# The first stage of a one-core attention layer: products of a cleared tile ahead of it, x's first tile in four loads, and loads issued when earlier ones have landed

## The chip, the cores and the metric

The kernel runs on one core of one Trainium2 chip. The metric is device microseconds of an execution, median of several. A core has TensorE (PE: matrix products; PEld in the profile is its weight load), VectorE (DVE), ScalarE (ACT), GpSimd (POOL) and SyncE (SP, which here only issues DMA transfers). ACT issues a few DMA transfers too.

## The reference, cut to what matters

x is 1024 tokens by 1024 features in float32. One projection gives queries, keys and values of three kinds of attention and a gate; each attention's output is normalised, gained, multiplied by the silu of the gate and projected back, and a layer norm of `alpha*x + y` ends it:

```python
h = jnp.einsum('bsd,de->bse', x, w_in[l]) + b_in[l]
qa, ka, va, qb, kb, vb, qc, z = jnp.split(h, split_idx, axis=-1)
mkv = jnp.einsum('bmd,de->bme', mem, w_mem[l])      # 256 memory tokens
y = jnp.concatenate([rms(oa), rms(ob), rms(oc)], -1) * g_branch[l] * silu(z)
x = layer_norm(DEEPNORM_ALPHA * x + y @ w_out[l], ln_gain[l], ln_bias[l])
```

Only the start of the projection is touched by the change: the product of x with the 256 columns of `vb`.

## The kernel before, in words

Every large float32 product is made of three: an operand is split into a high part (ACT rounds it: `x_hi`, `w_hi`, `mem_hi`, `g_hi`) and a low part (DVE subtracts: `x_lo`, `w_lo`, `mem_lo`), and PE adds hi*hi, hi*lo and lo*hi. The raw value and the low part share their memory.

**The first stage** is `first_chunk` (lines 680 to 701). The features are cut into KT = 8 tiles of 128. For each tile k PE goes over the 8 blocks of 128 tokens and issues three products of 128x256 each, so 24 products a tile and 192 in all, into four banks at once (`first_ps`). It waits ahead of each tile's weight piece (`FIRST_PIECES`: tiles 0, 1, 2-3, 4-7) and ahead of each half of x's tile, for both the rounding and the split. SP loads x as 16 pieces of 256 KB (two halves of each tile) with no wait between them (line 543); ACT issues the four weight pieces first of all (line 920), then loads its table of functions (L922).

**SP's queue behind x**, in this order (lines 544 to 551): chunk 1's weights (two of 512 KB, `load_chunk`), `ident`, `rope`, two broadcasts into `b_row`, chunk 2's weights (1 MB), `mem_raw` (1 MB), and, behind a wait for the end of the first stage, chunk 3's weights. All of these are one queue.

**ACT and DVE behind x**: ACT rounds chunk 1 (`kva`, from x), chunk 2 (`mk`, from the memory tokens) and the memory tokens (`memory_hi`). DVE makes the low parts in the same order (`chunk_lo(1)`, `chunk_lo(2)`, `memory_lo`), and only then runs `finish_first` (line 1131), which reads the first stage's four banks into `v_b`, and after that the jobs.

**The jobs** (`plan.steps`): PE computes one job after the other (`project`, lines 733 to 735 for a block of x, 24 products each), here job 0, job 1, keys 0, job 2, keys 1 and so on. `transpose_keys` (L749) waits for `keys_rotated`, which DVE gives at the end of `finish_keys` (L1215 to L1233) of that block. So the first transposition needs: `mem_raw` landed, `mem_hi`, `mem_lo`, `v_b`, and block 0's keys, in the order in which DVE has them written out.

Of the kernel before, what the change touches and what calls it, by code (L numbers as in the profile page):

```python
# [34 lines left out]
F32R = mybir.dt.float32r  # L35
ALU = mybir.AluOpType
ACT = mybir.ActivationFunctionType
AX = mybir.AxisListType

P = 128  # L40
SEQ = 1024
DM = 1024
MEM = 256
NB = SEQ // P
NBM = MEM // P
KT = DM // P
# [12 lines left out]
C = 256  # L59
HALF = 512  # L60
# [23 lines left out]
def units():  # L84

    out = []
    for i in range(NB):
# [6 lines left out]
        else:  # L94
# [8 lines left out]

GATE_ITERATIONS = 2
FIRST_PIECES = ((0, 1), (1, 2), (2, 4), (4, 8))
PREPARED = {3: (4, (5, 6, 6, 7)), 4: (8, (9, 9, 10, 10)), 5: (11, (11, 11, 12, 12)), 6: (13, (13, 13, 14, 14)),
            7: (18, (18, 19, 19, 20)), 8: (22, (22, 23, 23, 24)), "g0": (26, (27, 27)), "g1": (27, (28, 28))}
QS = 4
# [174 lines left out]
def layer(nc, x, x_t, mem_t, w_qkv, w_gate, w_mem, b_in, sinks, g_branch, w_out, ln_gain, ln_bias,  # L283
# [5 lines left out]
    with ExitStack() as ctx:  # L289
        def sem(name):  # L290
            return ctx.enter_context(nc.semaphore(name))
# [5 lines left out]
        spilled = [sem(f"spilled{s}") for s in range(2)]  # L297
        turned_keys_in, q_in = sem("turned_keys_in"), [sem(f"q_in{s}") for s in range(QS)]
        wo_in, ln_in = [sem(f"wo_in{k}") for k in range(FT)], sem("ln_in")
        x_in = [[sem(f"x_in{k}{h}") for h in range(2)] for k in range(KT)]  # L300
        first_in, mem_in = [sem(f"first_in{m}") for m in range(len(FIRST_PIECES))], sem("mem_in")
        chunk_in = [[sem(f"chunk_in{s}{h}") for h in range(2)] for s in range(3)]
        gate_in = [sem(f"gate_in{s}") for s in range(2)]
# [7 lines left out]
        x_rounded, chunk_rounded, chunk_split = sem("x_rounded"), sem("chunk_rounded"), sem("chunk_split")  # L311
        x_split, first_rounded, first_split = sem("x_split"), sem("first_rounded"), sem("first_split")
# [27 lines left out]
        def at(name, shape, dt, offset):  # L340
            return nc.alloc_sbuf_tensor_at(name, shape, dt, offset=offset)
# [7 lines left out]
        def nbytes(*shape):  # L349
            return 4 * int(np.prod(shape))  # L350
# [4 lines left out]
        x_hi = at("x_hi", [P, KT, SEQ], F32R, r_x.base)  # L355
        x_raw = at("x_raw", [P, KT, SEQ], F32, lo_half)
        x_lo = at("x_lo", [P, KT, SEQ], F32R, lo_half)
# [35 lines left out]

        r_t = Region(nbytes(2 * SEQ) + QS * nbytes(2, 2, P))
        prob = [at(f"prob{s}", [P, SEQ], F32, r_t.base + s * nbytes(SEQ)) for s in range(2)]
        spill = [at(f"spill{s}", [P, 2, 2, C], F32R, r_t.base + s * nbytes(SEQ)) for s in range(2)]
        q_at = r_t.base + nbytes(2 * SEQ)
        q_pair = [at(f"q_pair{s}", [P, 2, 2 * P], F32R, q_at + s * nbytes(2, 2, P)) for s in range(QS)]
# [45 lines left out]
        wide = [ctx.enter_context(nc.psum_tensor(f"wide{b}", [P, HALF], F32)) for b in range(3)]  # L444
# [5 lines left out]
        def f32(ap):  # L450
            return ap.bitcast(F32)
# [5 lines left out]
        def slot_of(c):  # L457
            return (c + 2) % 3
# [60 lines left out]
        def _(sp):  # L519
# [17 lines left out]
                sp.dma_start(g_raw[f % 2][:, :, :], w_gate[f]).then_inc(gate_in[f % 2], 16)  # L537


            for k in range(KT):  # L540
                for h in range(2):
                    cols = slice(h * HALF, (h + 1) * HALF)
                    sp.dma_start(x_raw[:, k, cols], x_t[k * P:(k + 1) * P, cols]).then_inc(x_in[k][h], 16)  # L543
            load_chunk(1)
            sp.dma_start(ident[:, :], ident_d).then_inc(ident_in, 16)
            sp.dma_start(rope[:, :, :], rope_d.rearrange("(b p) d -> p b d", p=P)).then_inc(rope_in, 16)
# [130 lines left out]

        @block.tensor
        def _(pe):
            def first_chunk():  # L680

                s = slot_of(0)
                for k in range(KT):
                    for m, (lo, _) in enumerate(FIRST_PIECES):
                        if lo == k:
                            pe.wait_ge(first_rounded, m + 1)
                            pe.wait_ge(first_split, m + 1)
                    for i in range(NB):
                        if i % (NB // 2) == 0:
                            pe.wait_ge(x_rounded, 2 * k + i // (NB // 2) + 1)  # L690
                            pe.wait_ge(x_split, 2 * k + i // (NB // 2) + 1)
                        cols = slice(i * P, (i + 1) * P)
                        dst = first_ps[i // 2][:, (i % 2) * C:(i % 2 + 1) * C]
                        pe.matmul(dst, x_hi[:, k, cols], w_hi[s][:, k, :], start=(k == 0 and i % 2 == 0),
                                  stop=False, skip_group_check=True)
                        pe.matmul(dst, x_hi[:, k, cols], w_lo[s][:, k, :], start=False, stop=False,
                                  skip_group_check=True)
                        mm = pe.matmul(dst, x_lo[:, k, cols], w_hi[s][:, k, :], start=False, stop=(k == KT - 1),
                                       skip_group_check=True)
                        if k == KT - 1 and i % 2:  # L700
                            mm.then_inc(first_full, 1)
# [36 lines left out]
            def transpose_keys(k):  # L738
# [10 lines left out]
                    t = pe.transpose(bank[:, h * P:(h + 1) * P], twice, ident[:, :])  # L749
                t.then_inc(narrow_full, 1)  # L750

            first_chunk()
            pe.wait_ge(ident_in, 16)
            for what, n in plan.steps:
# [161 lines left out]

        @block.scalar
        def _(act):
            for m, (lo, hi) in enumerate(FIRST_PIECES):
                act.dma_start(w_raw[slot_of(0)][:, lo:hi, :], w_qkv[COL_VB // C, :, lo:hi, :])\  # L920
                   .then_inc(first_in[m], 16)
            nc.scalar.preload_act_table_set("natural_log_exp_and_others")  # L922

            def chunk_hi(c):
# [9 lines left out]
                act.wait_ge(first_in[m], 16)  # L934
                act.activation(w_hi[s][:, k, :], w_raw[s][:, k, :], ACT.Copy).then_inc(first_rounded, 1)

            def x_hi_half(k, h):
                cols = slice(h * HALF, (h + 1) * HALF)
                act.wait_ge(x_in[k][h], 16)
                act.activation(x_hi[:, k, cols], x_raw[:, k, cols], ACT.Copy).then_inc(x_rounded, 1)  # L940

            def memory_hi():
                act.wait_ge(mem_in, 16)
# [34 lines left out]
            for k in range(KT):  # L978
                for m, (lo, _) in enumerate(FIRST_PIECES):
                    if lo == k:  # L980
                        first_hi(m)
                for h in range(2):
                    x_hi_half(k, h)
            chunk_hi(1)
            chunk_hi(2)
            memory_hi()
# [75 lines left out]
            for v in range(ITERATIONS):  # L1062
# [8 lines left out]
                f, since = divmod(v, 2 * GATE_ITERATIONS)  # L1071
# [4 lines left out]
                for i in stage_at(v, NORM_AT):  # L1076
                    s = i % 2
                    cols = slice(0, DM if i < NB - 1 else POOL_COLS)
# [5 lines left out]
                for i, j in stage_at(v, YSPLIT_AT):  # L1084
                    n = plan.narrow["y", i, j]
                    act.wait_ge(narrow_read[n % 2], n // 2 + 1)
                    f = slice(BRANCH_TILES[j][0], BRANCH_TILES[j][-1] + 1)
# [11 lines left out]
        def _(dve):  # L1099
# [4 lines left out]
                dve.tensor_tensor(w_lo[s][:, k, :], w_raw[s][:, k, :], f32(w_hi[s][:, k, :]), ALU.subtract)\  # L1104
                   .then_inc(first_split, 1)

            def x_lo_half(k, h):
                cols = slice(h * HALF, (h + 1) * HALF)
                dve.wait_ge(x_rounded, 2 * k + h + 1)
                dve.tensor_tensor(x_lo[:, k, cols], x_raw[:, k, cols], f32(x_hi[:, k, cols]), ALU.subtract)\  # L1110
                   .then_inc(x_split, 1)

            def chunk_lo(c, q):
# [122 lines left out]
            for k in range(KT):  # L1236
                for m, (lo, _) in enumerate(FIRST_PIECES):
                    if lo == k:
                        first_lo(m)
                for h in range(2):  # L1240
                    x_lo_half(k, h)
            for q in range(4):
                chunk_lo(1, q)
            for q in range(4):
# [120 lines left out]
            for v in range(ITERATIONS):  # L1365
# [8 lines left out]
                for i, j in stage_at(v, Y_AT):  # L1374
                    n, bank = bank_of(narrow, plan.narrow, ("y", i, j))
# [5 lines left out]
                for i in stage_at(v, NORM_AT):  # L1381
# [4 lines left out]
                    if i == NB - 1:  # L1386
                        cols = slice(POOL_COLS, DM)
# [6 lines left out]
                for half in range(2):  # L1394
                    for i in stage_at(v, RES_AT[half]):
                        cols = slice(half * HALF, (half + 1) * HALF)
# [10 lines left out]
                for i, j in stage_at(v, SCALE_AT):  # L1407
                    lo, n = BRANCHES[j]
# [8 lines left out]
        @block.gpsimd  # L1417
        def _(pool):
            def gate_lo(f):
                pool.wait_ge(gate_rounded, f + 1)  # L1420
                pool.tensor_tensor(g_lo[f % 2][:, :, :], g_raw[f % 2][:, :, :], f32(g_hi[f % 2][:, :, :]),  # L1421
                                   ALU.subtract).then_inc(gate_split, 1)

            for v in (v_a, v_b, v_c):
                pool.memset(v[:, :, :, HD:VW], 1.0).then_inc(ones_set, 1)
            for v in range(ITERATIONS):
                for i, j in stage_at(v, YSPLIT_AT):
                    pool.wait_ge(y_rounded, 3 * i + j + 1)
                    f, cols = slice(BRANCH_TILES[j][0], BRANCH_TILES[j][-1] + 1), slice(i * P, (i + 1) * P)
                    pool.tensor_tensor(y_lo[:, f, cols], zt[:, f, cols], f32(y_hi[:, i, f, :]), ALU.subtract)\  # L1430
                        .then_inc(y_split, 1)
                for i in stage_at(v, NORM_AT):
                    s = i % 2
                    cols = slice(0, DM if i < NB - 1 else POOL_COLS)
                    if i == 0:
                        pool.wait_ge(ln_in, 32)
                    pool.wait_ge(normed, i + 1)
                    pool.tensor_tensor(res[s][:, cols], res[s][:, cols], gain[:, cols], ALU.mult).then_inc(gained, 1)
                    pool.wait_ge(gained, i + 1)
                    pool.tensor_tensor(res[s][:, cols], res[s][:, cols], bias[:, cols], ALU.add).then_inc(finished, 1)  # L1440
                f, since = divmod(v, 2 * GATE_ITERATIONS)
                if since == GATE_ITERATIONS and 1 <= f < FT - 1:
                    gate_lo(f + 1)
# [73 lines left out]
```

## Time and profile before

| | us |
|---|---|
| median of 3 runs | 530.27 |
| the three runs | 530.27, 525.37, 530.83 |
| profiled execution, its own time | 525.63 |
| profiled execution, its span | 523.7 |
| PE busy in the span | 500.3 (96%) |
| DVE, ACT, POOL busy | 314.4, 226.0, 72.8 |

The span goes from the first instruction to the last; the execution's own time is 1.93 us longer. Views of the profile used below: the page (shares of the engines, the clock that was granted, the chain of work that ended last), the timeline of one engine, the sum of each engine's waits, the chain of waits in order of time, and the table of stretches of the span with the DMA engines' busy share and the rate that they moved. Products overlap in the timeline: the time that one takes out of PE's is the distance between two starts.

### The profile page before, as it was taken

How to read it: one execution, taken by the hardware profiler on the slowest of the kernel's cores; microseconds unless marked ns; L12 is line 12 of the kernel's file. 1: busy time of each engine (PE TensorE's matmuls, PEld its weight loads, DVE VectorE, ACT ScalarE, POOL GpSimd, SP SyncE). 2: the span in 40 equal slices, each digit the busy share in tenths (PEclk: the TensorE clock that was granted, in tenths of full speed). 3: DMA queues.
4: the chain of work that ended last, by engine and by line, in shares of the span. 5: the costliest groups of instructions: out<-in, count | busy, mean ns of one | idle time of the engine just before them, and what ended most of it. 6: DMA issues, size and time to landing. Idle time of an engine off the chain costs nothing.

```text
span 523.7 us, 9727 instructions
## 1 busy us (share of the span) xinstructions
PE 500.3 (96%) x3504; PEld 459.2 (88%) x3504; DVE 314.4 (60%) x872; ACT 226.0 (43%) x504; POOL 72.8 (14%) x53
## 2 busy tenths in 40 slices
PE   4999999999999989999999889999999999999993
PEld 4999999999999878888888778888888888998982
DVE  4786545467666434344535488876867676776534
ACT  5622212021212055554555478464547364454530
POOL 0000000000000001101111010241414140311415
PEclk9999999999999989999999999999999999999998
DMA  8952453467522543323213496133232324141022
GB/s 289 375 191 37 154 176 128 148 209 235 181 101 81 162 115 107 100 82 103 85 48 93 154 257 228 59 97 97 96 92 86 105 61 143 49 134 40 11 72 80
DMA packets 50030, 66.26 MB, mean 127 GB/s; under 512 B 9280, under 2 KB 39616, under 8 KB 49984
## 3 DMA queue, kind: packets, MB, share of 16 engines
q1 hardware_dynamic: 49408, 64.60, 39.2%
q10 hardware_dynamic: 576, 1.05, 0.6%
q8 instruction: 29, 0.48, 0.4%
q14 instruction: 17, 0.14, 0.1%
HBM read 50.41 MB, written 15.20 MB: 125 GB/s over the span
## 4 chain that ended last, share of the span: by engine, by line
PE 86%; DVE 4%; SPq 3%; DMA 3%; ACT 2%; issue 1%; POOLq 0%; POOL 0%; DVEq 0%; ACTq 0%
PE long_ps L889 16%; PE o_ps L856 13%; PE wide L722 7%; PE wide L724 7%; PE wide L723 7%; PE narrow L839 5%; PE long_ps L799 5%; PE long_ps L801 5%; PE long_ps L800 5%; PE wide L827 4%; PE wide L828 4%; DMA mem_raw<-in_mem_t 2%; PE narrow L866 2%; SPq L543 1%; PE wide L733 1%; PE wide L735 1%
## 5 line engine op out<-in xcount | busy, mean ns | idle before, releaser
L722 PE MATMUL wide<-x_hi,w_hi 128*128 128x256 f32 x320 | 88.5, 277 | 0.2
L723 PE MATMUL wide<-x_lo,w_hi 128*128 128x256 f32 x320 | 88.3, 276 | 0.0
L724 PE MATMUL wide<-x_hi,w_lo 128*128 128x256 f32 x320 | 88.3, 276 | 0.0
L722 PEld LDWEIGHTS wide<-x_hi,w_hi 128*128 128x128 f32 x320 | 60.1, 188 | 0.5 <-issue 0.5
L723 PEld LDWEIGHTS wide<-x_lo,w_hi 128*128 128x128 f32 x320 | 60.1, 188 | 0.0
L724 PEld LDWEIGHTS wide<-x_hi,w_lo 128*128 128x128 f32 x320 | 60.1, 188 | 0.0
L1043 ACT ACTIVATE prob_t<-narrow 128x512 f32<-128x512 f32 (+3 forms) x68 | 32.7, 505 | 56.1 <-PE narrow L839 56.0
L970 ACT ACTIVATE spill<-turn 128x512 fp32r<-128x512 f32 x21 | 13.3, 633 | 98.5 <-DVE turn L1188 72.7
L889 PE MATMUL long_ps<-wo_hi,y_hi 128*128 128x512 f32 x128 | 53.2, 416 | 0.0
L889 PE MATMUL long_ps<-wo_lo,y_hi 128*128 128x512 f32 x128 | 52.3, 409 | 0.0
L1421 POOL TENSOR_TENSOR g_lo<-g_raw,g_hi 128x1024 fp32r<-128x1024 f32 x6 | 14.3, 2386 | 272.1 <-ACT g_hi L975 272.1
L889 PE MATMUL long_ps<-wo_hi,y_lo 128*128 128x512 f32 x128 | 51.7, 404 | 0.0
L839 PE MATMUL narrow<-ident,prob 128*128 128x128 f32 x272 | 43.1, 274 | 4.1 <-ACT prob L1028 4.1
L799 PE MATMUL long_ps<-x_hi,g_hi 128*128 128x512 f32 x112 | 46.9, 419 | 0.0
L1028 ACT ACTIVATE prob<-prob,nb 128x128 f32<-128x128 f32 (+7 forms) x40 | 27.5, 698 | 39.8 <-DVE nb L1337 36.3
L801 PE MATMUL long_ps<-x_hi,g_lo 128*128 128x512 f32 x112 | 44.5, 398 | 0.0
L800 PE MATMUL long_ps<-x_lo,g_hi 128*128 128x512 f32 x112 | 44.5, 397 | 0.0
L1430 POOL TENSOR_TENSOR y_lo<-zt,y_hi 128x256 fp32r<-128x256 f32 (+1 forms) x24 | 22.1, 921 | 149.8 <-ACT y_hi L1088 149.8
L1028 ACT ACTIVATE prob<-wide,nb 128x128 f32<-128x128 f32 (+1 forms) x88 | 30.9, 406 | 20.5 <-DVE nb L1302 12.7
L856 PEld LDWEIGHTS o_ps<-v_b,prob_t 128*128 128x128 f32 x288 | 37.0, 191 | 2.7
L1354 DVE RECIPROCAL rden<-o_ps 128x1 f32<-128x1 f32 (+1 forms) x48 | 8.0, 166 | 50.1 <-PE o_ps L856 50.1
L839 PEld LDWEIGHTS narrow<-ident,prob 128*128 128x128 f32 x272 | 31.8, 140 | 5.9 <-ACT prob L1028 4.7
(151 smaller groups left out, 1204.4 us busy)
## 6 DMA issues: line engine op xcount, KB each, us to landing
q_spill<-spill SPq DMA_DIRECT2D x32, 256.0 KB, 2.5
q_pair<-q_spill SPq DMA_DIRECT2D x128, 64.0 KB, 2.0
w_raw<-in_w_qkv SPq DMA_DIRECT2D x12, 512.0 KB, 5.7
x_raw<-in_x_t SPq DMA_DIRECT2D x16, 256.0 KB, 7.9
g_raw<-in_w_gate SPq DMA_DIRECT2D x8, 512.0 KB, 3.5
q_pair<-q_spill SPq DMA_DIRECT2D x32, 128.0 KB, 2.7
q_pair<-q_spill SPq DMA_DIRECT2D x128, 32.0 KB, 1.8
wo_raw<-in_w_out SPq DMA_DIRECT2D x8, 512.0 KB, 4.6
```

Of the source, the lines that this page charges most:

```text
L722: pe.matmul(dst, w_hi[s][:, k, f], t_hi[:, k, cols], start=(k == 0), stop=False)
L723: pe.matmul(dst, w_hi[s][:, k, f], t_lo[:, k, cols], start=False, stop=False)
L724: mm = pe.matmul(dst, w_lo[s][:, k, f], t_hi[:, k, cols], start=False, stop=(k == KT - 1))
L799: pe.matmul(dst, g_hi[f % 2][:, k, :], x_hi[:, k, cols], start=(k == 0), stop=False)
L800: pe.matmul(dst, g_hi[f % 2][:, k, :], x_lo[:, k, cols], start=False, stop=False)
L801: mm = pe.matmul(dst, g_lo[f % 2][:, k, :], x_hi[:, k, cols], start=False, stop=(k == KT - 1))
L839: t = pe.transpose(bank[:, j * P:(j + 1) * P], prob[u % 2][:, col:col + P], ident[:, :])
L856: mm = pe.matmul(o_ps[:, at_col:at_col + VW], prob_t[w][:, col % HALF:col % HALF + P], v_tile(u, t, hh), start=(t == mine[0][0]), stop=(t ...
L889: mm = pe.matmul(long_ps[half][:, :], y, w[:, k, half * HALF:(half + 1) * HALF], start=(k == 0 and p == 0), stop=(n == half_done[half]))
L1028: e = act.activation(prob[s][:, cols], src, ACT.Exp, bias=nb[:, r, hh:hh + 1])
L1043: act.activation(prob_t[w % 4][:, 0:size], bank[:, 0:size], ACT.Copy).then_inc(narrow_read[n % 2], 1)
L1430: pool.tensor_tensor(y_lo[:, f, cols], zt[:, f, cols], f32(y_hi[:, i, f, :]), ALU.subtract)\
```

## The change

Six edits, all in the first stage. (1) POOL clears a tile `blank` of 128x256 ahead of its three other memsets, and PE, after a wait for that, issues 19 products of that tile into bank `wide0`, which the first job overwrites later. (2) x's tile 0 is loaded in four pieces of 128 KB rather than two of 256 KB; tiles 1 to 7 stay in halves, so SP issues 18 loads rather than 16. (3) Ahead of the loads of tile k, for k of 2 and more, SP waits until all pieces of tile k-2 have landed. (4) ACT issues weight pieces 0 and 1 first, piece 2 after the rounding of tile 0 and piece 3 after that of tile 1. (5) ACT and DVE round and split by the new pieces. (6) PE waits for a piece's rounding ahead of its first product, for the weight piece's low part ahead of the second, and for x's low part ahead of the third, where it waited for all of these ahead of the first.

```diff
+X_PIECES = [(0, lo, lo + C) for lo in range(0, SEQ, C)] \
+    + [(k, lo, lo + HALF) for k in range(1, KT) for lo in range(0, SEQ, HALF)]
+WARM_UP = 19
...
+        blank = at("blank", [P, C], F32R, r_t.base)
...
-            for k in range(KT):
-                for h in range(2):
-                    cols = slice(h * HALF, (h + 1) * HALF)
-                    sp.dma_start(x_raw[:, k, cols], x_t[k * P:(k + 1) * P, cols]).then_inc(x_in[k][h], 16)
+            for n, (k, lo, hi) in enumerate(X_PIECES):
+                if k >= 2 and lo == 0:
+                    for older, piece in enumerate(X_PIECES):
+                        if piece[0] == k - 2:
+                            sp.wait_ge(x_in[older], 16)
+                sp.dma_start(x_raw[:, k, lo:hi], x_t[k * P:(k + 1) * P, lo:hi]).then_inc(x_in[n], 16)
             load_chunk(1)
...
+            def warm_up():
+
+                pe.wait_ge(zeroed, 1)
+                for _ in range(WARM_UP):
+                    pe.matmul(wide[0][:, 0:C], blank[:, 0:P], blank[:, :], start=True, stop=True)
...
-                    for m, (lo, _) in enumerate(FIRST_PIECES):
-                        if lo == k:
-                            pe.wait_ge(first_rounded, m + 1)
-                            pe.wait_ge(first_split, m + 1)
+                    m = next((m for m, (lo, _) in enumerate(FIRST_PIECES) if lo == k), None)
+                    if m is not None:
+                        pe.wait_ge(first_rounded, m + 1)
                     for i in range(NB):
-                        if i % (NB // 2) == 0:
-                            pe.wait_ge(x_rounded, 2 * k + i // (NB // 2) + 1)
-                            pe.wait_ge(x_split, 2 * k + i // (NB // 2) + 1)
+                        n = piece_at.get((k, i * P))
+                        if n is not None:
+                            pe.wait_ge(x_rounded, n + 1)
...
+                        if i == 0 and m is not None:
+                            pe.wait_ge(first_split, m + 1)
                         pe.matmul(dst, x_hi[:, k, cols], w_lo[s][:, k, :], start=False, stop=False,
                                   skip_group_check=True)
+                        if n is not None:
+                            pe.wait_ge(x_split, n + 1)
...
+            warm_up()
             first_chunk()
...
-            for m, (lo, hi) in enumerate(FIRST_PIECES):
+            def load_first(m):
+                lo, hi = FIRST_PIECES[m]
                 act.dma_start(w_raw[slot_of(0)][:, lo:hi, :], w_qkv[COL_VB // C, :, lo:hi, :])\
                    .then_inc(first_in[m], 16)
+
+            load_first(0)
+            load_first(1)
             nc.scalar.preload_act_table_set("natural_log_exp_and_others")
...
-                for h in range(2):
-                    x_hi_half(k, h)
+                for n, piece in enumerate(X_PIECES):
+                    if piece[0] == k:
+                        x_hi_piece(n)
+                if k + 2 < len(FIRST_PIECES):
+                    load_first(k + 2)
...
+            pool.memset(f32(blank[:, :]), 0.0).then_inc(zeroed, 1)
             for v in (v_a, v_b, v_c):
                 pool.memset(v[:, :, :, HD:VW], 1.0).then_inc(ones_set, 1)
```

## Rows read from the trace of the kernel before

**Rows 1.** the page: busy time by engine, granted clock, and the chain that ended last.

```profile
PE 500.3 (96%) x3504; PEld 459.2 (88%) x3504; DVE 314.4 (60%) x872; ACT 226.0 (43%) x504; POOL 72.8 (14%) x53
...
PEclk9999999999999989999999999999999999999998
...
PE 86%; DVE 4%; SPq 3%; DMA 3%; ACT 2%; issue 1%; POOLq 0%; POOL 0%; DVEq 0%; ACTq 0%
```

**Rows 2.** timeline of PE, first stage and after: start us, duration us, engine, line, operation.

```profile
6.92 0.55 PE L694 MATMUL long_ps<-w_hi,x_hi 128*128 128x256 f32 x1 [6.92 <-DVE x_lo L1110]
...
12.17 0.28 PE L694 MATMUL long_ps<-w_hi,x_hi 128*128 128x256 f32 x1
...
31.22 0.28 PE L733 MATMUL wide<-w_hi,x_hi 128*128 128x256 f32 x1
...
36.55 0.28 PE L735 MATMUL wide<-w_hi,x_lo 128*128 128x256 f32 x1
37.08 0.44 PE L749 MATMUL narrow<-ident,keys 128*128 128x128 f32 x2 [0.26 <-DVE keys L1233]
```

**Rows 3.** waits of PE over the whole span: who for whom, us in total, times, longest.

```profile
PE narrow L839 <- ACT prob L1028: 4.1, 2, 2.7
```

**Rows 4.** the chain of waits in order of time, 0 to 60 us: start us, us, what.

```profile
11.34 5.80 SPq L547
...
18.61 10.95 DMA mem_raw<-in_mem_t
29.59 1.07 ACT mem_hi L946
...
33.18 2.40 DVE v_b L1136 x4
...
36.60 0.44 DVE keys L1233
```

**Rows 5.** stretches of the span, all engines, granted clock, DMA share, GB/s.

```profile
0.00:6.00 6.00, 0.00 (x0) 0.00 (x0) 0.42 (x1) 2.17 (x3) 0.46 (x7) 1.00 0.58 161
6.00:17.00 11.00, 10.08 (x67) 10.11 (x68) 9.11 (x15) 9.19 (x17) 0.00 (x0) 1.00 1.04 394
17.00:28.00 11.00, 11.00 (x99) 11.00 (x99) 6.91 (x12) 5.59 (x7) 0.00 (x0) 1.00 1.04 357
28.00:29.50 1.50, 1.50 (x15) 1.50 (x15) 1.29 (x2) 0.00 (x0) 0.00 (x0) 1.00 0.05 16
```

**Rows 6.** timeline of SP's DMA queue.

```profile
0.74 8.41 SPq L543 DMA_DIRECT2D x_raw<-in_x_t  x16
9.19 0.97 SPq L529 DMA_DIRECT2D w_raw<-in_w_qkv  x2
```

**Rows 7.** timeline of ACT, first stage.

```profile
5.11 0.42 ACT L935 ACTIVATE w_hi<-w_raw 128x256 fp32r<-128x256 f32 x1 [1.20 <-DMA w_raw<-in_w_qkv]
5.43 1.25 ACT L940 ACTIVATE x_hi<-x_raw 128x512 fp32r<-128x512 f32 x2
...
9.33 0.63 ACT L940 ACTIVATE x_hi<-x_raw 128x512 fp32r<-128x512 f32 x1 [1.05 <-DMA x_raw<-in_x_t]
```

**Rows 8.** timeline of DVE, low parts of the second chunk's weights.

```profile
20.15 2.64 DVE L1116 TENSOR_TENSOR w_lo<-w_raw,w_hi 128x512 fp32r<-128x512 f32 x4
```

**Rows 9.** DMA issues of the page, and x_raw by tile.

```profile
g_raw<-in_w_gate SPq DMA_DIRECT2D x8, 512.0 KB, 3.5
...
DMA to landing us min/median/max: 4.2/7.9/9.2
```

**Rows 10.** timeline of POOL, its memsets of the same kind.

```profile
0.79 0.16 POOL L1425 MEMSET v_b<- 128x64 f32 x1
```

**Rows 11.** timeline of PE, its last product.

```profile
515.24 0.40 PE L889 MATMUL long_ps<-wo_hi,y_lo 128*128 128x512 f32 x1
```

**Rows 12.** stretches of the span behind that product.

```profile
520.50:521.00 0.50, 0.00 (x0) 0.00 (x0) 0.00 (x0) 0.00 (x0) 0.50 (x1) 0.73 0.00 0
521.00:521.50 0.50, 0.00 (x0) 0.00 (x0) 0.00 (x0) 0.00 (x0) 0.15 (x1) 0.50 0.39 158
```

More of the change, by code:

```diff
@@ L299, in layer @@
         wo_in, ln_in = [sem(f"wo_in{k}") for k in range(FT)], sem("ln_in")
-        x_in = [[sem(f"x_in{k}{h}") for h in range(2)] for k in range(KT)]
+        x_in = [sem(f"x_in{n}") for n in range(len(X_PIECES))]
+        zeroed = sem("zeroed")
         first_in, mem_in = [sem(f"first_in{m}") for m in range(len(FIRST_PIECES))], sem("mem_in")
@@ L679, in _ @@
         def _(pe):
+            def warm_up():
+                pe.wait_ge(zeroed, 1)
+                for _ in range(WARM_UP):
+                    pe.matmul(wide[0][:, 0:C], blank[:, 0:P], blank[:, :], start=True, stop=True)
             def first_chunk():
                 s = slot_of(0)
+                piece_at = {(k, lo): n for n, (k, lo, _) in enumerate(X_PIECES)}
                 for k in range(KT):
-                    for m, (lo, _) in enumerate(FIRST_PIECES):
-                        if lo == k:
-                            pe.wait_ge(first_rounded, m + 1)
-                            pe.wait_ge(first_split, m + 1)
+                    m = next((m for m, (lo, _) in enumerate(FIRST_PIECES) if lo == k), None)
+                    if m is not None:
+                        pe.wait_ge(first_rounded, m + 1)
                     for i in range(NB):
-                        if i % (NB // 2) == 0:
-                            pe.wait_ge(x_rounded, 2 * k + i // (NB // 2) + 1)
-                            pe.wait_ge(x_split, 2 * k + i // (NB // 2) + 1)
+                        n = piece_at.get((k, i * P))
+                        if n is not None:
+                            pe.wait_ge(x_rounded, n + 1)
                         cols = slice(i * P, (i + 1) * P)
@@ L935, in first_hi, with x_hi_piece @@
                 act.activation(w_hi[s][:, k, :], w_raw[s][:, k, :], ACT.Copy).then_inc(first_rounded, 1)
[L937 to L940, printed above, removed]
+            def x_hi_piece(n):
+                k, lo, hi = X_PIECES[n]
+                act.wait_ge(x_in[n], 16)
+                act.activation(x_hi[:, k, lo:hi], x_raw[:, k, lo:hi], ACT.Copy).then_inc(x_rounded, 1)
             def memory_hi():
@@ L1105, in first_lo, with x_lo_piece @@
                    .then_inc(first_split, 1)
[L1107 to L1110, printed above, removed]
+            def x_lo_piece(n):
+                k, lo, hi = X_PIECES[n]
+                dve.wait_ge(x_rounded, n + 1)
+                dve.tensor_tensor(x_lo[:, k, lo:hi], x_raw[:, k, lo:hi], f32(x_hi[:, k, lo:hi]), ALU.subtract)\
                    .then_inc(x_split, 1)
@@ L1239, in _ @@
                         first_lo(m)
-                for h in range(2):
-                    x_lo_half(k, h)
+                for n, piece in enumerate(X_PIECES):
+                    if piece[0] == k:
+                        x_lo_piece(n)
             for q in range(4):
```

## The prediction

> **What bounds the kernel now.** The page first: PE is busy for 96% of the span and holds 86% of the chain that ended last, yet SP's queue and DMA hold 3% each [rows 1]. PE's timeline shows two speeds in the first stage: 24 products lie between 6.92 and 12.17, 0.219 us apart, and the other 168 between there and 31.22, 0.1134 us apart [rows 2]: the 1.2 GHz and the 2.4 GHz level. The granted-clock column reads 1.00 over both [rows 5], so at the start I go by the distances. From 31.22 PE does jobs 0 and 1, ends them at 36.83 (36.55 + 0.28), and waits 0.26 us for block 0's rotated keys [rows 2].
>
> That small wait matters. The chain in order of time passes not through the first stage's products but through SP's queue, the landing of `mem_raw`, its rounding at 29.59, `v_b` at 33.18 and the keys at 36.60 [rows 4]. DVE has `memory_lo` and `finish_first` written ahead of the first keys, so the transposition at 37.08 comes 7.5 us after `mem_raw` is there, whatever PE has done. Two bounds end within 0.3 us of each other here: PE's own work and the DMA engines. These moved 161 GB/s to 6.0, then 394 and 357 GB/s at a full share until 28.0, then next to nothing [rows 5]; `mem_raw` is used 1.6 us after they fall silent. Behind 37.1 PE is the bound to the end: its longest wait there is 2.7 us and its waits are few [rows 3].
>
> **The change, part by part.**
>
> *Warm-up.* POOL's memset of 64 columns takes 0.16 us [rows 10]. One of 256 columns is between that and four times that, 0.64; I take 0.4 (a fixed part is likely), so PE starts near 1.3. 19 products at 0.219 us end at 5.5. If the clock rises after as much work as before (5.25 us), it rises at 6.5. These products cost nothing: PE was idle to 6.92, and the bank is overwritten later.
>
> *Four pieces and split waits.* The weight's rounding started at 5.11 and took 0.42, x's two halves took 1.25 [rows 7]. A quarter takes about 0.35, so the first product can start at 6.0 rather than 6.92; with half the traffic ahead of it perhaps 0.8 earlier. Two products at half speed and 190 at 0.1134 give a stage that ends at 28.0: 3.2 us earlier (3.0 to 4.0). The next weights' low parts were done at 22.79 (20.15 + 2.64) [rows 8], so jobs 0 and 1 follow at once even if these come 4 us later, and PE stands at the first keys at 33.6.
>
> *Two more loads on SP* cost 2 x 0.53 us of issue (8.41 / 16) [rows 6], in SP's new waits. ACT's two moved issues, likely as long as SP's, lie between roundings. Late tiles have room: PE needs tile 7 at 25.3, and by the sum below it lands at about 19. Tile 2 is tight (needed at 11.7; it lands near 9.5, and three roundings of some 0.6 us leave it whole at 11.3); a stall of up to 1 us there is covered by the wait at the first keys. Should that cover be gone, it costs what it is.
>
> *SP's waits.* This is the edit that counts. Queued behind x's loads on SP are chunk 1, `ident`, `rope`, `b_row` twice, chunk 2 and `mem_raw`; the last one's reader is on the path. Up to the last byte of x and of the first weights there are 5.24 MB; before, they were through at 16.8 (6.0 x 161 + 10.8 x 394 GB/s), and the 4.0 MB behind them needed until 28.0 [rows 5]. After the change at most two tiles of x are under way. A cycle from a tile's landing to that of the tile two later: two issues 0.53 apart; a fixed part of 2.17, from the 3.5 us of a 512 KB load [rows 9] less 0.52 MB / 394 GB/s; 0.67 for the second half: 3.37, and I take 3.6 since the other tile's bytes share the engines. Tile 0 lands near 5.9 (its second half's rounding was the later half of the 1.25 us from 5.43). Tile 1's was rounded at 9.33 [rows 7], with 0.77 MB of weight pieces alongside that now come later: 7.4. So tiles 3, 5 and 7 are issued at 7.4, 11.0 and 14.6; tile 7 lands at 18.2, its last byte 1.5 before that, 16.7. The two late weight pieces (0.77 MB, 1.95 us) fall half into gaps: +1.0, so 17.7 to 17.8 against 16.8. From there the engines are full as before, so `mem_raw` and the first transposition come **1.0 us later**. The ends: with no gaps and the engines at 394 GB/s from 2.0 instead of the 232 that 161 over 6.0 comes to, 1.6 earlier; with a cycle of 4.7 (0.53 and x's shortest landing of 4.2 [rows 9]), tile 7 is issued at 16.8 and the shift is 4.2 later. I take 1.0, since the 512 KB loads are nearest in kind, and keep both ends. Here the Trainium skill speaks against the edit (DMA: Bandwidth & Descriptors, Anatomy of one DMA): each transfer has about 2.0 us of fixed time that its size doesn't change. By that figure the cycle would be 3.2 and the keys 0.3 us earlier, no loss at all; the measured 2.17 stands against it, and the wait is what exposes it.
>
> SP's issue of the rest is no new bound: `mem_raw` was issued 9.4 us after chunk 1, of which 5.8 were one blocked issue [rows 4, 6]. From 15.7 that gives 25.1 if it blocks again and 19.3 if not; its bytes are due near 26.
>
> **The sum.** Start and warm-up: -3.2 at the end of the stage, all of it turned into waiting at the first keys; those keys +1.0. The span goes from 523.7 to 524.7, and the execution's own time from 525.63 to 526.6. The median of the three runs is 4.6 above the profiled execution, so I add the 1.0 there: 531.3. The idle stretch at the first keys grows from 0.26 to 0.26 + 3.2 + 1.0 = 4.5 us.
>
> **The rivals.** *A: the clock falls in that stretch (the slower side).* After the last product (515.24 + 0.40 = 515.64 [rows 11]) the granted clock fell within 520.50 to 521.00, at 520.73 by its mean of 0.73 [rows 12]: 5.1 us after PE stopped. After the 2.7 us wait nothing is slower on the page [rows 1, 3]. 4.5 us lies between, nearer to 5.1. If it falls, the jobs behind the wait run 5.25 us at half speed, as at the start, which loses 24 x 0.106 = 2.5 us, on a path where PE is the bound: +3.5, 533.8; with the keys 2 us later, 534.8. It decides from an idle stretch of about 5 us, that is from a shift of 1.6, and with luck of timing below that. The Trainium skill (TensorE: Matmul & The Clock Gate, The HAM clock gate) has half speed as the default to which an idle engine goes back, which names this mechanism.
>
> *B: the gain goes through.* For that `mem_raw` would have to land earlier, or DVE not hold the keys. At its earliest (-1.6) it gives 528.7; the whole -3.2 (527.1) would need the chain to be misread, for which the 0.26 us wait, named after DVE's keys, leaves little room.
>
> *C: loads in turn starve the stage or delay the keys by 2.3 to 4.2*, clock held: 532.6 to 534.5.
>
> *D: the change doesn't do what it says*: the clock isn't up at the first true product. The stage would then end up to 2.5 us later, at 30.5, still ahead of the keys: the same 531.3, with a shorter idle stretch. It lies within the forecast.
>
> **How the numbers follow.** Forecast with D, 0.45 (shift -0.5 to +2.3, 529.8 to 532.6); A 0.30; B 0.15; C 0.10. The range has to hold these and the spread of the runs shown (525.4 to 530.8, so a median can lie 4 us lower for that alone): 526.0 to 535.5. It leaves out a low median with a gain, and C with A. 1% is 5.3 us, about what can be told from no change; no case alone reaches it on the faster side, so 0.10 for B with the runs' spread. Slower by as much takes A with C, or A with the spread: 0.12. Within: 0.78.
>
> **What would show it.** Right: 19 products of `blank` from about 1.3; first true product near 6.0, 0.113 us apart soon after; first job at about 28; DMA engines with gaps between 7 and 17; `mem_hi` at 30 to 32; a wait of PE at the first keys, for DVE, of 4 to 5 us; that transposition at about 38; behind it PE as before. A shows as products 0.21 to 0.22 us apart behind the wait, for some 5 us. It would be wrong if `mem_raw` landed clearly before 29, or PE's wait stayed under 2 us, or if what lies behind the first keys changed its length.

## The result, and the profile after

The change makes the kernel slower. The median is 539.75 us (536.69 to 542.19, 6 runs) against 527.82 (524.94 to 531.71, 6 runs); the ratio is 1.0201 [1.0157, 1.0245], some 10.6 us (1.0201 times 527.82; the two medians lie 11.9 apart). I had forecast 1.0 us more than before, 531.3, and a range up to 535.5. Ratios here and below are of fast runs alone; three slow ones of the kernel before, one of 1606 us, are left out.

The page of the changed kernel: span, busy time, and the chain's shares, to be held against [rows 1].

```profile
span 539.2 us, 9763 instructions
...
PE 510.6 (95%) x3523; PEld 469.0 (87%) x3523; DVE 314.7 (58%) x874; ACT 226.4 (42%) x506; POOL 73.1 (14%) x54
...
PE 85%; DMA 6%; DVE 4%; ACT 2%; SPq 2%; issue 1%; POOLq 0%; POOL 0%; DVEq 0%; ACTq 0%
```

PE's share stays near 95%, and DMA's share of the chain doubles from 3% to 6%. PE's waits over the whole span name the place at once; columns as in [rows 3].

```profile
PE narrow L766 <- DVE keys L1258: 10.5, 1, 10.5
...
PE wide L750 <- ACT w_hi L951: 0.6, 1, 0.6
```

The wait for the first rotated keys, 0.26 us before [rows 2], is 10.5 us. In the chain in order of time, up to that wait, one sees where it comes from; [rows 4] has the same view of before.

```profile
3.07 4.07 DMA x_raw<-in_x_t
...
7.58 6.57 DMA x_raw<-in_x_t
...
14.58 4.97 DMA x_raw<-in_x_t
...
20.46 0.44 SPq L534
...
25.42 13.16 DMA mem_raw<-in_mem_t
...
38.60 1.06 ACT mem_hi L968
...
45.61 0.44 DVE keys L1258
```

A second half of tile 1 issued at 3.07 lands at 7.14 and releases tile 3; tile 3's lands at 14.15 and releases tile 5; tile 5's lands at 19.55 and releases tile 7. Only then, at 20.46, does chunk 1 leave SP (9.19 before [rows 6]). `mem_raw` is issued at 25.42 and used at 38.60, against 29.59 [rows 4], and the keys come 9.0 us later, 7.5 us behind `mem_raw` as before. The stretches show the DMA engines part idle to 27 where they had been full [rows 5] (last three columns: granted clock, DMA share, GB/s):

```profile
6.00:12.00 6.00, 5.76 (x46) 5.58 (x46) 3.06 (x7) 3.07 (x7) 0.00 (x0) 1.00 0.80 264
12.00:17.00 5.00, 4.77 (x39) 4.58 (x40) 3.79 (x7) 3.56 (x6) 0.00 (x0) 1.00 0.80 265
17.00:22.00 5.00, 5.00 (x46) 5.00 (x46) 3.52 (x7) 2.53 (x4) 0.00 (x0) 1.00 0.63 206
22.00:27.00 5.00, 5.00 (x46) 5.00 (x46) 1.63 (x3) 1.23 (x2) 0.00 (x0) 1.00 0.86 248
27.00:32.00 5.00, 4.42 (x38) 4.25 (x37) 2.58 (x4) 2.12 (x2) 0.00 (x0) 1.00 1.01 312
32.00:37.00 5.00, 3.59 (x31) 3.38 (x29) 2.59 (x4) 2.12 (x2) 0.00 (x0) 1.00 1.06 383
```

PE itself did what was meant. Its timeline: warm-up at 1.10, first true product at 5.32 rather than 6.92 [rows 2], products 0.118 us apart from 6.8 on, a stall at tile 2, and the last product of the first stage at 28.84 (31.11 before). The first job waits for chunk 1's rounding until 29.70.

```profile
1.10 4.42 PE L691 MATMUL wide<-blank 128*128 128x256 f32 x19 [1.10 <-POOL blank L1450]
5.32 0.41 PE L707 MATMUL long_ps<-w_hi,x_hi 128*128 128x256 f32 x1
...
12.02 0.36 PE L707 MATMUL long_ps<-w_hi,x_hi 128*128 128x256 f32 x1 [0.25 <-ACT x_hi L962]
```

```profile
28.84 0.28 PE L715 MATMUL narrow<-w_hi,x_lo 128*128 128x256 f32 x1
29.70 0.36 PE L750 MATMUL wide<-w_hi,x_hi 128*128 128x256 f32 x1 [0.58 <-ACT w_hi L951]
```

```profile
46.09 0.69 PE L766 MATMUL narrow<-ident,keys 128*128 128x128 f32 x2 [10.51 <-DVE keys L1258]
```

The transposition of the first keys is at 46.09 (37.08 before), and the granted clock has fallen meanwhile (third column from the end):

```profile
35.00:40.00 5.00, 0.59 (x5) 0.38 (x4) 2.18 (x4) 1.95 (x3) 0.00 (x0) 1.00 1.05 391
40.00:45.00 5.00, 0.00 (x0) 0.00 (x0) 4.98 (x10) 0.61 (x1) 0.00 (x0) 0.58 0.47 88
45.00:50.00 5.00, 3.91 (x19) 3.91 (x20) 2.81 (x11) 0.39 (x1) 0.00 (x0) 0.50 0.18 49
50.00:55.00 5.00, 5.00 (x41) 5.00 (x41) 2.31 (x9) 0.57 (x2) 0.00 (x0) 0.89 0.00 0
```

From start times of the same instruction in both traces: the last product of the first stage is 2.3 us earlier than before, the first transposition 9.0 later, the product 60 places on 11.3 later. So 2.3 us are lost to half speed behind the wait. The profiled execution of after is 15.5 us longer than that of before; 4.1 of these come between 64 and 190 us, where PE issues its products at one of two paces, whatever the kernel (last section), and are not the change's. 9.0 + 2.3 = 11.3 us are, and the timed ratio says 10.6.

### The profile page after: what moved, and what is told of

Its sections match the earlier page's. It is cut to its first block, busy times and chain, and to the rows that moved or that the text cites. A ratio compares the mean times of both kernels' runs of the same rounds, so it can differ in the third digit from the quotient of the medians.

```text
span 539.2 us, 9763 instructions
## 1 busy us (share of the span) xinstructions
PE 510.6 (95%) x3523; PEld 469.0 (87%) x3523; DVE 314.7 (58%) x874; ACT 226.4 (42%) x506; POOL 73.1 (14%) x54
## 4 chain that ended last, share of the span: by engine, by line
PE 85%; DMA 6%; DVE 4%; ACT 2%; SPq 2%; issue 1%; POOLq 0%; POOL 0%; DVEq 0%; ACTq 0%
PE long_ps L907 16%; PE o_ps L874 12%; PE wide L741 7%; PE wide L739 7%; PE wide L740 7%; PE narrow L857 5%; PE long_ps L817 5%; PE long_ps L819 5%; PE long_ps L818 4%; PE wide L845 4%; PE wide L846 4%; DMA x_raw<-in_x_t 3%; DMA mem_raw<-in_mem_t 2%; PE narrow L884 2%; PE wide L750 2%; PE wide L751 2%
## 5 line engine op out<-in xcount | busy, mean ns | idle before, releaser
L741 PE MATMUL wide<-x_hi,w_lo 128*128 128x256 f32 x320 | 89.6, 280 | 0.0
L992 ACT ACTIVATE spill<-turn 128x512 fp32r<-128x512 f32 x21 | 13.3, 632 | 103.0 <-DVE turn L1213 76.1
```

What stands on the lines that cost most here:

```text
L741: mm = pe.matmul(dst, w_lo[s][:, k, f], t_hi[:, k, cols], start=False, stop=(k == KT - 1))
```

## The experiments

Two theories after the result. **W**: SP's waits delay everything queued behind x; `mem_raw` is ahead of the first keys in DVE's order; the clock falls in the wait that opens. **R**: the warm-up, the small loads or the late weight pieces cost the time. "Keys" below is the start of the first key transposition.

| kernel | `mem_hi` starts | keys | median us | ratio to before |
|---|---|---|---|---|
| before | 29.59 | 37.08 | 527.82 to 530.68 by batch | 1 |
| changed | 38.60 | 46.09 | 539.75 | 1.0201 [1.0157, 1.0245] |
| e1_no_sp_wait | 30.18 | 37.67 | 529.87 | 1.0022 [0.9984, 1.0060] |
| e2_only_sp_wait | 35.00 | 42.49 | 538.29 | 1.0183 [1.0120, 1.0245] |
| e3_only_warm_up | 29.77 | 37.39 | 529.64 | 0.9989 [0.9950, 1.0027] |
| e4_filled_wait | 35.99 | 44.48 | 535.31 | 1.0156 [1.0078, 1.0234] |
| e5_keys_first | 39.56 | 35.85 | 529.25 | 0.9974 [0.9941, 1.0007] |
| e6_keys_first_before | | 36.40 | 529.94 | 1.0015 [0.9980, 1.0049] |
| e7_four_tiles | 29.87 | 37.36 | 531.02 | 1.0018 [0.9990, 1.0046] |
| e8_best | 38.04 | 34.37 | 527.86 | 0.9956 [0.9921, 0.9992] |
| e9_chunk3_held | 38.35 | 45.83 | 541.81 | 1.0225 [1.0169, 1.0281] |
| e10_best_no_warm_up | | 35.58 | 528.44 | 0.9966 [0.9922, 1.0010] |
| e11_longer_warm_up | | 36.68 | 525.21 (one run) | |

Starts are from one trace each. In e5, e6, e8 and e10 `mem_hi` is late because ACT's order puts it there. Each ratio is against the runs of the kernel before in its own batch, so two kernels' ratios are compared with less certainty than each with before.

**e1: the changed kernel without SP's waits.**

```diff
-                if k >= 2 and lo == 0:
-                    for older, piece in enumerate(X_PIECES):
-                        if piece[0] == k - 2:
-                            sp.wait_ge(x_in[older], 16)
```

> The changed kernel without SP's waits ahead of x's loads of tiles 2 to 7; all else as changed (warm-up, four pieces, ACT's later weight pieces, split waits). Theory W (SP's waits delay everything queued behind x, and with it mem_raw and the first rotated keys, which the jobs need): x's last load is issued by 10.5, mem_hi starts at 29.6 +- 0.7 (38.6 in the changed kernel), the first key transposition is at 37.1 +- 0.7 (46.1), PE waits 3 to 4 us there, and the time is within 2 us of the kernel before, or 2.3 us more if the clock falls in that wait. Rival R (the warm-up, the four small loads or ACT's later weight pieces cost it): mem_hi stays at 35 or later and the time stays 6 us or more above the kernel before.

As W expects: `mem_hi` back to 30.18, keys at 37.67, no difference from before. R falls. One number was missed: PE waited 1.1 us at the keys, not 3 to 4, since the late weight piece 2 held tile 2 to 14.05 and the stage's last product was only 0.2 us earlier than before.

```profile
PE narrow L762 <- DVE keys L1254: 1.1, 1, 1.1
```

**e2: the kernel before with SP's waits alone.**

```diff
             for k in range(KT):
+                if k >= 2:
+                    for h in range(2):
+                        sp.wait_ge(x_in[k - 2][h], 16)
```

> The kernel before with one addition: SP waits, ahead of the two loads of x's tile k (k from 2), for both halves of tile k-2. Theory W: x's last load is issued at 18 to 21 rather than 9.1, mem_hi starts at 37 to 39, the first key transposition is at 45 to 47 rather than 37.1, the clock falls in PE's wait ahead of it and costs some 2.3 us more; 9 to 12 us above the kernel before, ratio 1.017 to 1.023. Rival R: under 4 us above it.

The waits alone make the loss: 1.0183. The chain was shorter than expected (chunk 1 leaves SP at 18.09, keys at 42.49: 5.4 later, not 8 to 10), PE waited 6.0 us at the keys, the half-speed stretch behind that took 1.7 us more, and the profiled execution is 10.9 longer, 4.1 of it again in the stretch to 190 us. The timed ratio says more (9.7 us) than 5.4 + 1.7; a single trace of such a kernel places the landing to 2 or 3 us only: with the same loads as in the changed kernel, `mem_hi` starts 2.6 us earlier in e4's.

```profile
PE narrow L752 <- DVE keys L1236: 6.0, 1, 6.0
```

**e3: the kernel before with the warm-up alone** (the cleared tile, POOL's memset and the 19 products, as in the change).

> The kernel before with the 19 products of a cleared tile alone. Both W and R in its form for the loads: first job's first product at 28 to 29 (31.22 before), all of that turned into a longer wait at the first keys (2.5 to 3.5 us rather than 0.26), transposition at 37.1 +- 0.3, time within 1 us of the kernel before. Rival (the warm-up itself costs): 2 us or more slower.

No cost and no gain, as expected, but not for the reason given: the first job came at 31.95, not 28 to 29, and the longer wait at the keys never opened. In PE's timeline the 19 products end at 5.5, PE is idle for 1.7 us, and the true ones run 0.21 us apart until 13.3:

```profile
1.09 4.42 PE L756 MATMUL wide<-blank 128*128 128x256 f32 x19 [1.09 <-POOL blank L1429]
7.21 0.55 PE L696 MATMUL long_ps<-w_hi,x_hi 128*128 128x256 f32 x1 [1.70 <-ACT w_hi L940]
...
12.47 0.41 PE L696 MATMUL long_ps<-w_hi,x_hi 128*128 128x256 f32 x1
12.68 0.41 PE L698 MATMUL long_ps<-w_lo,x_hi 128*128 128x256 f32 x1
```

**e4: the changed kernel with its long wait filled.**

```diff
+                if k == 0:
+                    for _ in range(80):
+                        pe.matmul(wide[2][:, 0:C], blank[:, 0:P], blank[:, :], start=True, stop=True)
                 pe.wait_ge(keys_rotated, k + 1)
```

> The changed kernel with 80 more products of the cleared tile, into a free bank, ahead of PE's wait for the first rotated keys (80 x 0.113 = 9.1 us within its 10.5 us wait). Theory H (the clock fell during that wait and the jobs behind it ran 5 us at half speed): keys still at 46 +- 1, granted clock 1.00 from 40 to 60, products behind the wait 0.113 to 0.118 apart at once, and 2.3 us less than the changed kernel: ratio to the kernel before 1.014 to 1.018. Rival (the slow products behind the wait have another cause): no gain, ratio 1.020 or more.

The filler and the transposition behind it, then the stretches around them:

```profile
34.88 9.76 PE L761 MATMUL wide<-blank 128*128 128x256 f32 x80
44.48 0.38 PE L770 MATMUL narrow<-ident,keys 128*128 128x128 f32 x2
```

```profile
40.00:45.00 5.00, 5.00 (x44) 5.00 (x43) 4.74 (x16) 0.10 (x1) 0.00 (x0) 1.00 0.29 59
45.00:50.00 5.00, 5.00 (x45) 5.00 (x45) 2.33 (x8) 0.67 (x2) 0.00 (x0) 1.00 0.02 5
50.00:55.00 5.00, 5.00 (x46) 5.00 (x45) 3.17 (x13) 2.66 (x4) 0.00 (x0) 1.00 0.00 0
```

The clock stays up, and the shift at the keys (+7.40) is the shift 60 places on (+7.42), where the changed kernel loses 2.3 between the two. H stands by the trace. The ratio, 1.0156, agrees but can't show it: its interval overlaps that of the changed kernel, and the 2.6 us earlier landing is in it too. The other kernels line up with H. Where PE waited 1.1, 1.3 and 2.5 us for the first keys (e1, e7, e11), the shift against before changed by 0.1 us or less over the next 60 places; where it waited 6.0 us (e2), it grew by 1.7; where it waited 10.5 (changed, e9), by 2.3. The filler ended 0.9 us after the keys were ready (35.99 + 7.5 = 43.5), so it cost a little too.

**e5: the changed kernel, with the keys ahead of the memory tokens.** DVE and ACT only:

```diff
             for q in range(4):
                 chunk_lo(1, q)
-            for q in range(4):
-                chunk_lo(2, q)
-            for q in range(4):
-                memory_lo(q)
             finish_first()
...
                 if what == "job":
+                    if n in (2, 3):
+                        for q in range(2 * n - 4, 2 * n - 2):
+                            chunk_lo(2, q)
+                    if n in (4, 5):
+                        for q in range(2 * n - 8, 2 * n - 6):
+                            memory_lo(q)
```

and `memory_hi()` moved behind the second `keys_hi`.

> The changed kernel, SP's waits and all, with another order on two engines: DVE reads the first stage's banks and does the first jobs ahead of the low parts of chunk 2 and of the memory tokens (which follow jobs 2 to 5), and ACT rounds the memory tokens after the second keys. Theory W (the late loads cost time only through mem_raw and chunk 2 being ahead of the first keys in DVE's and ACT's order): mem_hi still starts at 35 or later, yet the first key transposition comes at 34 to 36 and PE waits under 1 us for it; no fall of the clock before 60 us; 1.5 to 2.5 us below the kernel before (ratio 0.995 to 0.997). Rival L (the late loads hold PE elsewhere too, or the warm-up costs): 3 us or more above it.

```profile
35.85 0.44 PE L766 MATMUL narrow<-ident,keys 128*128 128x128 f32 x2
```

SP's waits are all there (chunk 1 leaves at 19.83), and the 10 us are gone: 0.9974 [0.9941, 1.0007]. So the late loads cost time only through the order in which DVE and ACT do their work; the run changes both and doesn't tell one from the other. Against before the gain is 1.2 us in the trace at that point, less than the 1.5 to 2.5 expected, and not told from none by the times.

**e6: the same order in the kernel before.**

> The kernel before with the same new order on DVE and ACT alone. Both theories: PE stands at the first keys at 36.8 and waits 0.26 us there, so the order frees at most that: 0 to 0.3 us, no difference. It shows what e5_keys_first owes to the order itself. Rival: the first keys' wait hides more than its 0.26 us, 1 us or more gained.

No difference, as expected: PE is the bound there by then. In the profiled executions of e5 and e6, unlike that of before, the granted clock also falls between 315 and 325 us (its mean from 320 to 325 is 0.80 and 0.78), and these stretches take 1.9 and 1.6 us longer. In e8 and e10, with the same order, it doesn't, so the order isn't shown to be the cause.

**e7: the changed kernel with `k - 4` for `k - 2`** (and `k >= 4`).

> The changed kernel with SP waiting for tile k-4 rather than k-2, so up to four tiles of x under way. Theory W: the DMA engines hardly run dry, x's last load is issued by 13 to 15 (20.4 with two tiles), mem_hi starts at 30 to 32 (38.6), first key transposition at 37.5 to 39.5, time 0.5 to 3 us above the kernel before, and up to 2.3 more if the clock falls. Rival (any wait of SP costs about the same): 8 us or more above it.

Last x load issued by 11.8, `mem_hi` at 29.87, 1.0018. It is not the waiting as such but having only two tiles under way. The last load and the landing both came a little earlier than expected (13 to 15, and 30 to 32).

**e9: the changed kernel, chunk 3 held.**

```diff
+            sp.wait_ge(mem_in, 16)
             load_chunk(3)
```

> The changed kernel with SP waiting for mem_raw's landing ahead of chunk 3's loads (in the changed kernel these, released by the earlier end of the first stage, were issued at 29.2 while mem_raw was still being moved). Theory C (chunk 3's 1 MB took part of the engines ahead of mem_raw's last bytes): mem_raw's time from issue to landing 9.5 to 11.5 us rather than 13.2, first keys 1 to 2 us earlier than in the changed kernel, ratio to the kernel before 1.014 to 1.018. Rival (one queue is served in order and chunk 3 costs nothing): 13 us, ratio 1.020.

Theory C falls: it asked for 9.5 to 11.5 us from issue to landing. The chain of this kernel:

```profile
8.30 6.50 DMA x_raw<-in_x_t
...
15.23 4.00 DMA x_raw<-in_x_t
...
25.69 12.64 DMA mem_raw<-in_mem_t
...
38.35 1.06 ACT mem_hi L969
```

`mem_raw` takes 12.6 us although nothing is behind it, so by these two traces chunk 3 accounts for about half a microsecond of the 13.2. The lines also repeat the two long flights of x, 6.5 and 4.0 us.

**e8: a version meant to beat both.** e5's order, `k - 3` for `k - 2`, and weight piece 2 issued at the start.

> The order of e5_keys_first, SP waiting for tile k-3, and ACT issuing weight piece 2 at the start with pieces 0 and 1. Theory W: PE never waits over 0.5 us in the first stage or at chunk 1 (in the changed kernel tile 2 and chunk 1 cost 1.3 us together), the first job's first product comes at 27.7 to 28.5 (31.22 before), the first keys behind it with no wait, and the time is 2.5 to 3.5 us below the kernel before (ratio 0.993 to 0.995). Rival L: no gain, since something later takes it.

0.9956 [0.9921, 0.9992]: faster than before by 0.1 to 0.8%, and by the two ratios some 2.4% faster than the changed kernel. Against before that is 2.3 us, a little under the 2.5 to 3.5 expected. The first job starts at 28.92 rather than 27.7 to 28.5 and PE still waited 0.9 us for x's rounding in the first stage.

**e10: e8 without the warm-up.**

> e8_best without the cleared tile and its 19 products. Theory: once nothing behind the first stage covers it, the warm-up is worth what it saves of half-speed products, at most 2.5 us less the stalls that it meets: first job's first product at 29.8 to 31 (28.9 in e8_best), 1 to 2 us above e8_best, ratio to the kernel before 0.998 to 1.000. Rival (the warm-up is worth nothing even there): as e8_best, 0.9956.

In the traces the stage's last product is 1.2 us later than in e8 (30.02 against 28.81). The times (0.9966 against 0.9956, where 0.998 to 1.000 was expected) can't tell these apart: that the warm-up is worth anything in the time is not shown.

**e11: e3 with 28 products for 19.**

> e3_only_warm_up with 28 products of the cleared tile rather than 19. In e3_only_warm_up PE was idle from 5.5 to 7.2 between the last of them and the first true product, and the clock rose only at 13.1. Theory G (that idle stretch kept it down): with products until the first true one is ready, the clock rises by 6 to 9 us and the first stage ends some 2 us earlier. Rival P (products of zeros don't raise the clock, or it was chance): it rises at 12 to 13 again.

```profile
1.10 5.39 PE L756 MATMUL wide<-blank 128*128 128x256 f32 x28 [1.10 <-POOL blank L1429]
6.59 0.36 PE L696 MATMUL long_ps<-w_hi,x_hi 128*128 128x256 f32 x1
6.79 0.28 PE L698 MATMUL long_ps<-w_lo,x_hi 128*128 128x256 f32 x1
6.92 0.28 PE L700 MATMUL long_ps<-w_hi,x_lo 128*128 128x256 f32 x1
```

Theory G fits: no idle stretch, full pace from the second true product, the stage 2.6 us earlier than before. All of it but 0.4 becomes waiting at the keys (36.68, a wait of 2.5 us). It is one execution, and when the clock rises differs between executions by more than 2 us (last section), so chance, Rival P, is not excluded.

## Why the prediction was wrong

- **The bound was read rightly.** The chain through SP's queue, `mem_raw` and DVE's order to the first keys is where the time went, and a faster first stage alone bought only a wait (e11: stage 2.6 us earlier, keys 0.4 earlier). In e3 and e1 the stage itself gained 0.2 us at most.
- **The step that failed is the size of SP's waits: +1.0 us forecast, +9.0 measured**, beyond the upper end of 4.2. Two terms of it. *The cycle* from a tile's landing to that of the tile two later was put at 3.6 us, its fixed part from the 3.5 us of `g_raw` loads. It measured 7.0 and 5.4 (7.14 to 14.15 to 19.55), so chunk 1 left at 20.46, not near 15.7. These 4.8 us are the larger part of the 8.0 missed. The row taken was of 512 KB loads elsewhere in the kernel; here four to six loads, weight pieces among them, were under way. That their sharing of the engines makes the flights long is likely and not isolated by a run. x's own landings, 4.2 to 9.2 us [rows 9], were the nearer rows, and I used the shortest of them only as the far end. *What is behind x* was taken to move at 357 GB/s as before, 11.2 us for 4.0 MB. It took from 22 to about 37, some 15 us, at 248 and 312 GB/s up to 32; that is the other 3.2 us. e9 leaves about half a microsecond of it to chunk 3. That small loads (`ident`, `rope`, `b_row`) no longer lay in a deep queue fits the 206 and 248 GB/s rows, but no run isolates it: open.
- **Rival A's mechanism came true**, at the size given: 2.3 us lost (2.5 worked out), with the idle stretch at 10.5 us rather than 4.5. e4 shows it. It had been a rival, with 0.30, because of the wrong size above.
- **One reading in A was false.** I wrote that after the 2.7 us wait nothing is slower. The kernel before has a half-speed stretch right there, at 186, and the 8 in the `PEclk` row of [rows 1] is that stretch; its stretches:

```profile
180.00:184.00 4.00, 2.35 (x12) 1.84 (x10) 0.88 (x4) 0.00 (x0) 0.00 (x0) 1.00 0.63 196
184.00:186.00 2.00, 0.97 (x7) 0.89 (x8) 0.02 (x1) 1.83 (x4) 0.00 (x0) 1.00 0.34 82
186.00:190.00 4.00, 4.00 (x13) 3.15 (x12) 0.99 (x4) 1.73 (x4) 0.00 (x0) 0.57 0.76 222
```

  PE stood still once in them, for 2.7 us. So "it decides from about 5 us" was too high a bar. Nor does the length of the wait decide alone: behind the same 2.7 us wait the granted clock falls in ten of the thirteen profiled executions and stays up in three, those of e4, e7 and e8. Stretches of e8, its wait from 184.3 to 187.0:

```profile
184.00:188.00 4.00, 1.34 (x10) 1.11 (x9) 0.69 (x1) 1.88 (x4) 0.00 (x0) 1.00 0.58 148
188.00:192.00 4.00, 3.01 (x17) 2.46 (x16) 1.17 (x5) 1.69 (x4) 0.00 (x0) 1.00 0.69 221
```

- **The warm-up** saved 2.3 us at the end of the stage, not 3.2: the stall at tile 2, whose weight piece came late, took back 1.0. Behind the stage chunk 1's rounding held the first job for another 0.7. That the warm-up costs nothing held (e3).
- **The fixed time of a transfer.** The Trainium skill (DMA: Bandwidth & Descriptors, Anatomy of one DMA) has about 2.0 us, and states it for transfers that GpSimd issues, where these are issued by SP. By that figure the cycle would be 3.2 us, an estimate; the 7.0 and 5.4 measured disagree with it further than with my row. That waiting exposes each transfer's own time, as I wrote, was right in direction.
- **The range** failed for the same step: C, the case of later keys, ended at 4.2, and was never joined to A, although a later landing lengthens the very wait on which A depends.

## What to carry to other kernels

Before a load is made to wait for another, list what is queued behind it and find the reader of the last of these; price the cycle by landings measured under the same traffic, not by loads elsewhere in the kernel. Where two bounds end within a fraction of a microsecond, a gain on one buys only a longer wait, and a wait of PE can cost its clock as well. Here the cure was on another engine: let DVE do the work that PE needs next ahead of work whose data comes late.

## What the runs showed of the hardware

**Two paces at full clock.** Between 84 and 165 us PE issues the same kind of projection products in every kernel, without a wait. From 70 to 170 us some 885 of them fit in one execution and 847 in another; before, changed, and e4, in this order (e4 has a short gap ahead of 80 and then before's pace):

```profile
70.00:170.00 100.00, 100.00 (x885) 100.00 (x884) 60.00 (x130) 20.88 (x28) 0.00 (x0) 1.00 0.47 154
```

```profile
70.00:170.00 100.00, 99.84 (x847) 99.50 (x846) 54.42 (x116) 19.87 (x27) 0.00 (x0) 1.00 0.52 168
```

```profile
70.00:170.00 100.00, 99.84 (x877) 99.49 (x876) 58.56 (x127) 20.72 (x29) 0.00 (x0) 1.00 0.52 168
```

The granted clock is 1.00 in all. Start to start it is 0.1133 us (before, e4, e11) or 0.1178 us (the ten other profiled executions), which comes to 4.1 us by 190 us. The pace holds from about 80 us to the end of these products. It doesn't go with the change: e4 has it fast, e1 slow. The kernel before has times near 525 and, more often, near 530; that the pace makes that gap is likely (its profiled execution, 525.63, is fast), but runs without a profile can't show it. Its cause is open. A lone pair of profiles can show 4 us that are no change's; only what lies outside that stretch, or the timed ratio, counts.

**When the clock rises differs between executions.** The 19 products of zeros are the same in each of these kernels, start at 1.1, and run 0.21 us apart until the clock rises:

| kernel | the 19 products take | PE idle behind them | true products at full pace from |
|---|---|---|---|
| changed, e1, e9, e4 | 4.42 | 0 to 0.26 | 6.5 to 7.2 |
| e5, e8 | 4.05, 4.08 | 0.52, 0.31 | 6.3, 6.1 |
| e7 | 3.82 | 1.52 | 7.0 |
| e3 | 4.42 | 1.70 | 13.3 |

Where they take less than 4.42 us, the clock had risen before they ended. In e7 it then stayed up through 1.5 us of idleness:

```profile
1.10 3.82 PE L691 MATMUL wide<-blank 128*128 128x256 f32 x19 [1.10 <-POOL blank L1450]
6.43 0.36 PE L707 MATMUL long_ps<-w_hi,x_hi 128*128 128x256 f32 x1 [1.52 <-ACT x_hi L962]
```

In e3 it hadn't risen when PE went idle for 1.7 us, and the warm-up was lost. So what these traces show is that a warm-up is lost when a gap comes before the rise, and not that any gap of such a length loses it; each row is one execution.
